# Squares of x eight tiles behind its split, and the norm product moved inside the third unit

## What is computed

```python
def _rmsnorm(x, g):
    xf = x.astype(jnp.float32)
    y = xf * lax.rsqrt(jnp.mean(xf * xf, axis=-1, keepdims=True) + EPS) * g.astype(jnp.float32)
...
    h = _rmsnorm(x, norm_gain) @ w_in
    u, z_a, q, k, v, z_b, g_a, g_b = jnp.split(h, SPLITS, axis=-1)
```

## Time and profile before

| | |
|---|---|
| median of 3 runs | 1566.88 us (1566.75 to 1567.06) |
| the profiled execution | 1566.93 us, span 1565.1 us |
| TensorE busy | 1543.8 us, 99% of the span |
| VectorE busy | 658.1 us (42%) |
| ScalarE busy | 421.7 us (27%) |
| GpSimd busy | 480.1 us (31%) |
| granted TensorE clock, mean | 0.996 |

### The profile page before, as it was taken

How to read it: one execution, slowest core, us unless ns; L and a number is a source line. 1 busy time by engine, 2 the same in 40 slices (tenths; PEclk the granted TensorE clock), 3 DMA queues, 4 the chain that set the end, 5 groups by cost and what they waited for, 6 DMA issues and landing times.

```text
span 1565.1 us, 21895 instructions
## 1 busy us (share of the span) xinstructions
PE 1543.8 (99%) x8605; PEld 1335.4 (85%) x8605; DVE 658.1 (42%) x1032; ACT 421.7 (27%) x576; POOL 480.1 (31%) x117
## 2 busy tenths in 40 slices
PE   7999999999999999999999999998999999999999
PEld 6999888999999878878787787878988888888887
DVE  7697771248884142333424334248603224500000
ACT  7312332421111313323233332315411111311110
POOL 4333232323332323222322223222333323333331
PEclk9999999999999999999999999998999999999999
DMA  7524449634224354464544555446234424332440
GB/s 272 138 83 156 140 144 177 223 133 135 85 99 143 100 133 119 126 150 127 149 115 109 146 141 123 127 155 223 80 126 144 141 89 148 114 132 73 144 148 34
DMA packets 166635, 209.26 MB, mean 134 GB/s; under 512 B 106640, under 2 KB 124848, under 8 KB 152880
## 3 DMA queue, kind: packets, MB, share of 16 engines
q1 hardware_dynamic: 63840, 133.85, 28.3%
q10 hardware_dynamic: 102736, 74.57, 16.0%
HBM read 162.99 MB, written 42.76 MB: 131 GB/s over the span
## 4 chain that ended last, share of the span: by engine, by line
PE 96%; DVE 1%; ACT 1%; issue 1%; DMA 0%; SPq 0%; ACTq 0%
PE ps L774 34%; PE ps L471 24%; PE ps L869 14%; PE ps L564 9%; PE ps L777 8%; PE ps L709 1%; PE ps L686 1%; PE ps L687 1%; PE ps L695 1%; DVE ssum L1383 1%; PE ps L671 1%; PE ps L545 1%; PE ps L735 0%; PE ps L702 0%; PE ps L703 0%
## 5 line engine op out<-in xcount | busy, mean ns | idle before, releaser
L438 POOL TENSOR_TENSOR w_lo<-raw,w_hi 128x2048 fp32r<-128x2048 f32 (+1 forms) x111 | 479.5, 4321 | 1060.1 <-ACT w_hi L902 1060.1
L902 ACT ACTIVATE w_hi<-raw 128x2048 fp32r<-128x2048 f32 (+1 forms) x111 | 196.8, 1776 | 711.2 <-PE ps L777 291.7
L774 PE MATMUL ps<-x_hi,w_hi 128*128 128x512 f32 x512 | 205.2, 401 | 0.0
L774 PE MATMUL ps<-x_hi,w_lo 128*128 128x512 f32 x512 | 199.8, 390 | 0.0
L774 PE MATMUL ps<-x_lo,w_hi 128*128 128x512 f32 x512 | 199.5, 390 | 0.0
L471 PE MATMUL ps<-x_hi,w_hi 128*128 128x320 f32 x768 | 176.7, 311 | 11.1 <-DVE x_lo L1376 11.1
L471 PE MATMUL ps<-x_lo,w_hi 128*128 128x320 f32 x768 | 175.6, 310 | 0.0
L471 PE MATMUL ps<-x_hi,w_lo 128*128 128x320 f32 x768 | 175.4, 310 | 0.0
L471 PEld LDWEIGHTS ps<-x_hi,w_hi 128*128 128x128 f32 x768 | 128.5, 189 | 12.9 <-issue 9.9
L471 PEld LDWEIGHTS ps<-x_hi,w_lo 128*128 128x128 f32 x768 | 129.0, 188 | 0.0
L471 PEld LDWEIGHTS ps<-x_lo,w_hi 128*128 128x128 f32 x768 | 128.8, 188 | 0.0
(11 more groups left out here) (254 smaller groups left out, 2469.3 us busy)
## 6 DMA issues: line engine op xcount, KB each, us to landing
raw<-in_wts SPq DMA_DIRECT2D x99, 1024.0 KB, 4.9
g_scr<-gbuf ACTq DMA_DIRECT2D x8, 1024.0 KB, 8.0
gate_in<-g_scr ACTq DMA_DIRECT2D x8, 1024.0 KB, 6.0
x_raw<-in_xT SPq DMA_DIRECT2D x16, 320.0 KB, 7.8
z_scr<-E ACTq DMA_DIRECT2D x16, 320.0 KB, 2.2
Y<-in_x_tok ACTq DMA_DIRECT2D x20, 256.0 KB, 4.6
out_y_tok<-Y ACTq DMA_DIRECT2D x20, 256.0 KB, 2.7
c_scr<-powers SPq DMA_DIRECT2D x16, 256.0 KB, 4.3
```

The source lines that it names most:

```text
L438: return nc.gpsimd.tensor_tensor(w_lo[p][:, cols], raw[p][:, cols], w_hi[p][:, cols].bitcast(F32), ALU.subtract)
L774: last = nc.tensor.matmul(ps[:, bank, :], w[p][:, col + P * i:col + P * i + P], act[:, 0:PROMPT], start=opens, stop=final and w is w_lo)
L902: return nc.scalar.activation(out, in_, func, **kw)
```

## The change

Three orders change and nothing else is computed:

- ScalarE squares tile k-8 where it squared tile k; of the last eight squares, tiles 8 to 11 come before the two copies `u_raw`, tiles 12 to 15 behind them, and so does the last quarter of `w_hi` of unit 2.
- VectorE splits ten tiles of x before its first addition and makes the last eight additions in a row at the end.
- TensorE does the norm products in front of tile k = 8 of unit 2 (the third unit).

`u_raw` moves to other addresses, because x is still read when it is written.

```diff
+SQ_LAG = 8
...
+                if k == 8:
+                    norm_sums()
...
-            pe.wait_ge(small_loaded, SMALL * 16)
-            nc.tensor.matmul(ps[0:16, 6, 0:RELW], tab[:], hot[:], start=True, stop=True).then_inc(rel_ready, 1)
-            pe.wait_ge(ssum_done, 1)
-            pe.wait_ge(prep, 2)
-            sum_squares(ssum, 4, ones).then_inc(ss_ready, 1)
-            for t in range(TT):
-                last = nc.tensor.matmul(ps[:, 7, t:t + 1], ssum[:, P * t:P * t + P], ones[:, 0:1], start=True, stop=True)
-            last.then_inc(tok_ready, 1)
+            def norm_sums():
...
...
+            def square_x(k):
+                if k == 0:
+                    A(ssum[:], x_raw[:, 0, :], ACT.Square).then_inc(x_sq, 1)
+                else:
+                    if k > 2:
+                        act.wait_ge(dve_step, k - 2)
+                    A(sq[k % 2][:], x_raw[:, k, :], ACT.Square).then_inc(x_sq, 1)
...
                 A(x_hi[:, k, :], x_raw[:, k, :], ACT.Copy, scale=gcol[:, k:k + 1]).then_inc(x_hi_done, 1)
-                if k == 0:
...
+                if k >= SQ_LAG:
+                    square_x(k - SQ_LAG)
+
+            hi_part2(2)
+            for k in range(KT - SQ_LAG, KT - 4):
+                square_x(k)
             for p in range(2):
                 act.wait_ge(proj_done, p + 1)
                 A(halves(u_raw[p][:]), acc(p), ACT.Copy).then_inc(acc_free, 1)
+            hi_part2(3)
+            for k in range(KT - 4, KT):
+                square_x(k)
...
+            for k in range(KT):
+                dve.wait_ge(x_hi_done, k + 1)
+                v.scalar_tensor_tensor(out=x_lo[:, k, :], in0=x_raw[:, k, :], scalar=gcol[:, k:k + 1],
+                                       in1=x_hi[:, k, :].bitcast(F32), op0=ALU.mult,
+                                       op1=ALU.subtract).then_inc(x_split, 1)
+                if k >= SQ_LAG:
+                    add_square(k - SQ_LAG)
+            for k in range(KT - SQ_LAG, KT):
+                add_square(k)
```

More of the change, by code:

```diff
@@ L132, in build @@
     x_raw = at("x_raw", M, [P, KT, TOK])
-    u_raw = [at(f"u_raw{i}", M + 640 * (14 + i), [P, TOK]) for i in range(2)]
+    u_raw = [at(f"u_raw{i}", (E + 1280, S + 1152)[i], [P, TOK]) for i in range(2)]
     powers = at("powers", M, [P, BLK, 2, 2, (STEP + 1) * CH])
@@ L517, in _ @@
                         last.then_inc(part_used, 1)
-            pe.wait_ge(small_loaded, SMALL * 16)
-            nc.tensor.matmul(ps[0:16, 6, 0:RELW], tab[:], hot[:], start=True, stop=True).then_inc(rel_ready, 1)
-            pe.wait_ge(ssum_done, 1)
-            pe.wait_ge(prep, 2)
-            sum_squares(ssum, 4, ones).then_inc(ss_ready, 1)
-            for t in range(TT):
-                last = nc.tensor.matmul(ps[:, 7, t:t + 1], ssum[:, P * t:P * t + P], ones[:, 0:1], start=True, stop=True)
-            last.then_inc(tok_ready, 1)
+            def norm_sums():
+                pe.wait_ge(small_loaded, SMALL * 16)
+                nc.tensor.matmul(ps[0:16, 6, 0:RELW], tab[:], hot[:], start=True, stop=True).then_inc(rel_ready, 1)
+                pe.wait_ge(ssum_done, 1)
+                pe.wait_ge(prep, 2)
+                sum_squares(ssum, 4, ones).then_inc(ss_ready, 1)
+                for t in range(TT):
+                    last = nc.tensor.matmul(ps[:, 7, t:t + 1], ssum[:, P * t:P * t + P], ones[:, 0:1],
+                                            start=True, stop=True)
+                last.then_inc(tok_ready, 1)
             def ssm_mats(i):
@@ L1371, in _, with add_square @@
             st = Steps(dve, dve_step)
[L1374 to L1378, removed]
+            def add_square(k):
                 dve.wait_ge(x_sq, k + 1)
```

## The result

| | before | after |
|---|---|---|
| median | 1567.05 us (1566.64 to 1568.1, 8 runs) | 1571.84 us (1571.19 to 1573.01, 8 runs) |
| profiled execution | 1566.93 us, span 1565.1 us | 1571.19 us, span 1569.4 us |

The ratio of after to before is 1.003, with a 95% interval of 1.002 to 1.0041: the change costs about 4.8 us. The forecast was 1569.2 us and its range ended at 1571.2 us; the sign was right and the size was not.

The account below looks back on a forecast made before the run. VectorE's chain behind `rinv` was taken to release TensorE at unit 6: 2.7 us delay less 0.45 slack, rounded 2.3 us later, carried from 1566.93 to 1569.2 us. Likeliest case 1568.5 to 1569.9 us, range 1565.8 to 1571.2 us.

Parts of the forecast that it names:

- The `x_lo` waits: TensorE in units 0 and 1: no tile waits after the start, units end at 37.7, 4.7 us gained.
- the delay of the norm products: Inside unit 2: they start at 45.1 instead of 42.40, moving everything that hangs on `rinv` 2.7 us later.
- the start of unit 2: TensorE waits for the copy `u_raw[0]` behind ScalarE's squares and goes on at 38.05, 0.3 us lost.
- rival 2: Units 0 and 1: GpSimd's pieces make the last square late, chain delay 3.7, +3.3 us, 1570.2 us; chance 0.12.
- it moves rigidly: From `rinv` through the store of `E[0]` to VectorE's evacuations: the whole chain shifts by 2.7 us.
- the slack: Before unit 6: its start less the end of `evac_u(4)`, 0.45 us in the kernel before, the tightest point.
- Unit 3: TensorE ready at 54.9, weights at 55.2: wait 0.3 us.
- Unit 4: TensorE ready at 69.3, accumulator released by `evac_u(2)` at 72.4: wait 3.1 us.
- Unit 5: TensorE ready at 86.5, accumulator released by `evac_u(3)` at 87.4: wait 0.9 us.
- Unit 6: TensorE ready at 101.5, accumulator released by `evac_u(4)` at 103.8: wait 2.3 us.
- Rival 1: Unit 6: after the idle gap TensorE restarts at half clock, 1.6 us more, +3.9 us, 1570.8 us; chance 0.2.
- Rival 3: Store of `E[0]` lands much sooner than 11.5 us after issue; at most -2.4 us, 1564.5 us; chance 0.08.

Follow-up runs that it names:

- e1: Kernel after with the norm products in front of tile 12 of unit 2 instead of tile 8: 1576.58 us.
- e3: Kernel after with no lag of the squares (0 instead of 8), norm products still before tile 8 of unit 2: 1575.22 us.
- e9: Kernel after with lag 3 instead of 8, all squares before the copies, norm products before tile 1 of unit 2: 1567.15 us.
- e5: Kernel after with sixteen unused 128x128 matmuls keeping TensorE busy before its first tile: 1571.65 us.
- e7: Kernel after with a third buffer for `E`, so that `evac_u(2)` no longer waits for the first store to land: 1570.09 us.
- e6: Kernel before with sixteen unused 128x128 matmuls keeping TensorE busy before its first tile: 1568.64 us.
- e12: Kernel after with the 1 MB bias table write moved from before the store of `E[0]` to behind the load of unit 6: 1565.52 us.
- e8: Kernel after with `evac_u(4)` at step 1 instead of 4 and `evac_u(7)` at step 2 instead of 3 of their power computations: 1573.41 us.
- e4: Kernel after with VectorE's `evac_u(4)` at step 1 of `mats(0)` instead of step 4: 1574.17 us.

## Why the prediction was wrong

**Right.** The `x_lo` waits all go. VectorE's last `x_lo` is done at 34.3 (33 to 34 forecast). The additions end at 45.2, before TensorE asks for them. The lead of TensorE isn't worth anything, because units 4 and 6 are released by VectorE, and VectorE's clock is set by `rinv`; unit 6 is where it is decided. The kernel after, e1, e3 and e9 show this chain with the norm products at four different moments. The loss goes to the end undiminished (+3.93 at unit 6, +4.26 in the profiled execution).

**The step that failed** is the delay of the norm products, 2.7 us, and in it the start of unit 2: "the last square ends at about 37.2", "so the copy starts at 37.1 to 37.5 and TensorE goes on at 37.9 to 38.2". Measured: the square of tile 11 ends at 37.71, the copy starts at 38.23, unit 2 at 38.99. That is 0.94 of the 1.13 us by which the delay was undersized (3.83 for 2.7); the other 0.2 us lie in the eight tiles, 7.24 for 7.05.

Two things make unit 2 late, and each covers the other. The first is the ring of squares and additions, which I had run through too fast: a square waits for the addition that frees its buffer, and the last three start 0.93 us apart (0.74 and 0.19 of waiting). The square of tile 11 ends at 37.71 here and at 38.0 to 38.4 in e1, e5 and e7, where ScalarE and VectorE do the same in the same order, and not at 37.2. The second is TensorE's cold start, which I took from the trace before: the row at 11.31 was the first warm one there, but in the trace after it is that at 13.98, eleven cold rows and not six. In the kernel after TensorE is the later of the two by the 0.52 us that the copy waits for it. e7 separates them. Its code is the same until 60 us, and in its profiled execution only five rows were cold; there unit 2 waits for the copy behind the square:

```profile
38.77 0.56 PE L472 MATMUL ps<-x_hi,w_hi 128*128 128x320 f32 x2 [0.87 <-ACT u_raw L907]
```

and its norm products start at 46.00, in e5, without cold rows, at 45.91: 3.6 and 3.5 us later than before. So of the 1.13 us the ring alone makes 0.8 to 0.9, and the longer cold start adds 0.2 to 0.3 in the execution that was profiled. The ring is the mechanism of rival 2 (copy behind the last square, delay 3.7, forecast 1570.2), to which I had given 0.12; that GpSimd's pieces were the reason for the late square, as rival 2 says, was not tested.

**A smaller miss** is "it moves rigidly". The store's landing took 12.1 us for 11.5, and `evac_u(4)` moved by 4.29, not by 3.83. e6 shows that the landing is no constant (13.1 us there), and that what exceeds the slack passes on. The sum with both measured terms is 4.29 - 0.45 = 3.84 at unit 6, where 3.93 was measured; so the frame of the sum stands and two of its terms were too small. (The slack was also read a little too large: unit 6 starts 0.15 us after `evac_u(4)` ends, 105.48 for 105.33, which the 0.45 us leave out.) These terms explain the 4.3 us of the profiled execution; the median is another 0.5 us higher, see below.

**The waits, one by one.** Unit 3: 0.3 forecast and met, though the table of waits has no line for it: the last row of unit 2 starts at 55.80, unit 3 0.61 us later and not 0.29, right behind its weights (done at 56.35). Unit 4: 3.1 forecast, 3.44. Unit 5: 0.9 forecast, none, since TensorE ran cold through the start of unit 4 and came later by itself. Unit 6: 2.3 forecast, 1.36, for the same reason, with a start at 105.48 and not 103.8. The measured waits alone would give -3.1 (`x_lo`) + 4.8 (`E`) = +1.7 us at unit 6, where +3.93 was measured: the slow rows at the start and in unit 4 are no waits. The clock time of the release takes them in.

**Rival 1, the cold clock.** The clock fell to 0.50 in unit 4, where it filled the later waits and cost nothing, as the text said. It did not fall at unit 6 in the profiled execution of the kernel after, behind 1.36 us without work. In e1, with 2.19 us in front of unit 6, it did, for 1.4 us; in e5 and e7, with the same 2.19 us, it did not (1.00 through the whole unit). So the length of the gap alone does not decide it. The Trainium skill (TensorE: Matmul & The Clock Gate, HAM oscillation) describes a kernel in which every wait between two bursts of matmuls brings the half clock back; the rows agree at unit 4 and in e1 and disagree in e5 and e7, and that the sum would be this rival's by that page, as the prediction has it, took the page too far. Of the 4.26 us of the profiled execution nothing is due to this rival. For the other executions that is open, see below.

**Rival 3, an earlier landing,** did not come by itself. But its mechanism is real, as e12 shows: it gives 1565.52 us, where the rival was priced at 1564.5.

**What stays open.** The median of the kernel after lies 0.65 us above its profiled execution; where the other executions lose more isn't known, since only one was profiled. It is the fastest of the eight and has the highest mean granted clock of them, 0.997; the other seven have 0.994 to 0.997, most of them 0.994 or 0.995, where the kernel before has 0.996 to 0.998 beside e1 to e4. So slow spells of TensorE, rival 1 at unit 6 among them, may well be in the 0.65 us; no trace shows it. How long the start stays cold differs between executions (five to eleven rows), and the store's landing too; what sets either was not tried. Nor was e12's edit tried on the kernel before.

## What to carry to other kernels

When a change lets one engine run ahead, don't count the waits it removes: list the releases it gets from other engines, with the clock time and the slack of each, and see what the change does to the smallest (here 0.45 us at unit 6, against the 3.4 us by which TensorE came sooner to unit 2), and then to the next ones, since a lead won at one release can be lost at the one behind it (e5, e8). A product that heads a long chain should not be moved later to hide a wait in front of it. And where an engine idles long for a transfer, look at what else is being moved at that time before giving it another buffer: here the neighbour was worth 6.3 us and the buffer 1.7.

## What the runs showed of the hardware

- A write of 1 MB from 16 partitions took 14.6 us to land (14.4 in e12). From 64 to 70 us, while it ran, the 16 DMA engines were busy for 0.88 of the time at 95 GB/s (window below, of the kernel after). A store of 320 KB issued beside it landed in 12.1 us and not 2.5, and ScalarE's two DMA issues took 4.91 us and not 1.48, which held up all of ScalarE's later work. Whether the 16 partitions make the write slow was not tried.

```profile
64.00:70.00 6.00, 6.00 (x44) 6.00 (x42) 0.00 (x0) 3.43 (x3) 2.35 (x1) 1.00 0.88 95
```

- A VectorE multiplication of 128x512 with two SBUF inputs took 5.05 us instead of 0.69 beside a GpSimd instruction of 4.61 us that had begun 0.11 us before it (e4), 4.4 us more, nearly the whole length of the other. The Trainium skill (GPSIMD Engine Reference, Specifications) says that the two engines share their SBUF interfaces when VectorE reads two SBUF inputs; the trace agrees, and shows the size of it. In e7 even a 128x32 operation, begun at 68.95, took 3.13 us, to the end of GpSimd's piece at 72.0.
- The first rows of two matmuls stood 0.53 us apart, as they do elsewhere in this case at a granted clock of 0.50, and 0.29 later: six rows in the trace before, eleven in the trace after, five in e7, whose code is the same up to there. The clock column of the profile reads 1.00 for them (8.0 to 13.5 us), so the half clock is inferred from the distances.
